# Transposed probabilities of the neighbourhood attention, copied by the scalar and the vector engine in halves

## What is computed

```python
def neighborhood_attention(q, k, v, rpb):
    ...
    qb = q.reshape(B, H, rows, n_cb, Q_BLOCK_W, dh)
    kg = k[:, :, tok]
    vg = v[:, :, tok]
    s = jnp.einsum('bhrnqd,bhrnkd->bhrnqk', qb, kg).astype(jnp.float32) * (dh ** -0.5)
    bias = rpb.astype(jnp.float32)[:, ri, ci]
    s = jnp.where(mask[None, None, None], s + bias[None], NEG)
    p = jax.nn.softmax(s, axis=-1)
    o = jnp.einsum('bhrnqk,bhrnkd->bhrnqd', p.astype(v.dtype), vg)
    return o.reshape(B, H, T, dh)
```

## Time and profile before

| | us |
|---|---|
| median of 3 runs | 1976.39 |
| lowest, highest | 1972.84, 1978.12 |
| profiled execution | 1976.45 |
| its span, first to last instruction | 1974.7 |
| neighbourhood attention, layer 0 | 313.0 to 353.1 |
| neighbourhood attention, layer 1 | 1276.8 to 1317.6 |

### The profile page before, as it was taken

One profiled execution on the slowest core, in us unless ns is written; L12 is line 12 of the kernel. 1 busy time (PEld: TensorE's weight loads), 2 busy tenths in 40 slices (PEclk: granted clock), 3 DMA queues, 4 the chain that ended last, 5 costly groups with the idle time before them and its releaser, 6 DMA issues.

```text
span 1974.7 us, 29955 instructions
## 1 busy us (share of the span) xinstructions
PE 1617.4 (82%) x9962; PEld 972.8 (49%) x9962; DVE 935.2 (47%) x1825; ACT 324.1 (16%) x690; POOL 291.9 (15%) x402
## 2 busy tenths in 40 slices
PE   3998897955997878997849988978399789998874
PEld 1474445853554445554426634467355455554441
DVE  3866757144443333443367476643533344343334
ACT  1242236020000000000032323341000000000000
POOL 0003221001211111121100141300101111111110
PEclk9999998977999999999979999989599999999997
DMA  8951252642999999899488214424369999999995
GB/s 258 312 162 44 85 150 86 256 171 96 381 396 412 405 409 406 358 407 408 191 276 273 75 42 146 154 118 185 131 267 408 408 407 391 412 402 408 410 398 205
DMA packets 150930, 538.59 MB, mean 273 GB/s; under 512 B 16942, under 2 KB 109342, under 8 KB 117566
## 3 DMA queue, kind: packets, MB, share of 16 engines
q1 hardware_dynamic: 135440, 514.17, 67.8%
q0 software_dynamic: 11520, 16.82, 2.6%
q10 hardware_dynamic: 3888, 6.61, 1.0%
HBM read 533.34 MB, written 25.20 MB: 283 GB/s over the span
## 4 chain that ended last, share of the span: by engine, by line
PE 47%; DMA 31%; DVE 8%; issue 6%; SPq 5%; ACT 2%; DVEq 0%; POOL 0%; POOLq 0%; ACTq 0%
PE bank L564 43%; DMA ring<-w 17%; DMA pool_b<-w 7%; DMA pool_a<-xn_rows,tok_now 2%; DMA y_rows<-pool_a,row_now 2%; PE bank L856 2%; DMA pool_b<-b_ada 2%; SPq L430 1%; DVE low L1254 1%; PE bank L878 1%; DVE ring L1433 1%; SPq L415 1%; ACT pool_a L1136 1%; DMA pool_a<-y_rows 1%; SPq L414 1%
## 5 line engine op out<-in xcount | busy, mean ns | idle before, releaser
L564 PE MATMUL bank<-ring,pool_a 128*64 128x256 f32 (+2 forms) x3968 | 557.7, 445 | 112.2 <-DMA ring<-w 67.4
L564 PEld LDWEIGHTS bank<-ring,pool_a 128*64 128x64 f32 (+1 forms) x3968 | 294.7, 143 | 353.3 <-issue 193.8
L564 PE MATMUL bank<-hT,ring 128*128 128x512 f32 (+1 forms) x672 | 304.3, 609 | 32.9 <-DVE pool_b L1418 29.3
L1693 DVE TENSOR_SCALAR pool_a<-pool_a 128x256 f32<-128x256 f32 x72 | 21.4, 297 | 590.2 <-ACT pool_a L1165 590.2
L564 PEld LDWEIGHTS bank<-hT,ring 128*128 128x128 f32 (+1 forms) x672 | 126.9, 192 | 194.2 <-issue 158.2
L1165 ACT ACTIVATE pool_a<-bank 128x256 f32<-128x256 f32 x72 | 27.6, 383 | 1041.5 <-PE bank L564 1041.5
L564 PE MATMUL bank<-ring,hT 128*128 128x256 f32 x768 | 168.6, 380 | 1.9 <-ACT hT L1150 1.9
L564 PEld LDWEIGHTS bank<-ring,hT 128*128 128x128 f32 x768 | 144.9, 190 | 25.7 <-issue 6.4
L1694 DVE RECIPROCAL pool_a<-pool_a 128x256 f32<-128x256 f32 x72 | 126.2, 1753 | 2.5
L1706 DVE TENSOR_TENSOR pool_a<-bank,g_bc 64x512 f32<-64x512 f32 x144 | 99.2, 689 | 40.6 <-PE bank L564 36.4
L564 PE MATMUL bank<-hT,pool_a 128*64 128x256 f32 x768 | 92.8, 396 | 22.0 <-DMA hT<-w 22.0
(11 more groups left out here) (272 smaller groups left out, 1564.1 us busy)
## 6 DMA issues: line engine op xcount, KB each, us to landing
ring<-w SPq DMA_DIRECT2D x129, 2048.0 KB, 26.1
pool_b<-w SPq DMA_DIRECT2D x22, 2048.0 KB, 25.6
hT<-w SPq DMA_DIRECT2D x22, 2048.0 KB, 21.1
low<-w SPq DMA_DIRECT2D x22, 2048.0 KB, 23.0
ring<-w_ada SPq DMA_DIRECT2D x40, 1024.0 KB, 12.1
ring<-w_in SPq DMA_DIRECT2D x24, 1024.0 KB, 5.8
pool_b<-w_ada SPq DMA_DIRECT2D x16, 1024.0 KB
ring<-w_out SPq DMA_DIRECT2D x8, 1024.0 KB, 10.5
```

The lines of the kernel that those rows point to most:

```text
L564: return nc.tensor.matmul(out, lhsT, rhs, start=start, stop=stop, skip_group_check=True)
L1693: own(V.tensor_scalar(e1, e1, 1.0, None, ALU.add), t, 2)
```

## The change

Of the two PSUM tiles of transposed probabilities of each head, the scalar engine goes on copying i = 0, and the vector engine copies i = 1, in its loop two heads after the scores, behind the scaling of the head before. The vector loop gets a tenth turn for the last head. Both engines wait explicitly, from head 2 on, for the product that last read the half of `PT_sb` that they overwrite, and the matrix engine waits for the last copy of each engine before a product. The count order of emptied tiles is adapted.

```diff
         if d >= 1:
-            t += [(("PT", 2 * d - 2 + r, i), "a") for r in range(2) for i in range(2)]
+            t += [(("PT", 2 * d - 2 + r, i), "ad"[i]) for r in range(2) for i in range(2)]
...
             return index[("S", key[1] - 1, 1)] + 0.5
+        if key[0] == "PT" and key[2] == 1 and key[1] < 6:
+            return index[("S", key[1] + 2, 1)] + 0.3
         return index[key]
...
                         d = n - 2
-                        pe.wait_ge(act_took.s, act_took.at(l, taken[("PT", 2 * d + 1, 1)][1]))
+                        pe.wait_ge(act_took.s, act_took.at(l, taken[("PT", 2 * d + 1, 0)][1]))
+                        pe.wait_ge(dve_took.s, dve_took.at(l, taken[("PT", 2 * d + 1, 1)][1]))
...
                     if 2 <= h < 10:
                         g = h - 2
-                        for i in range(2):
-                            b = tile(("PT", g, i))
-                            F(PT_sb[:, g % 2, 2 * i:2 * i + 2, :].rearrange("p c n -> p (c n)"), b[:, :], ACT.Copy
-                              ).then_inc(act_took.s, 1)
+                        b = tile(("PT", g, 0))
+                        if g >= 2:
+                            act.wait_ge(on_done.s, on_done.at(l, g // 2))
+                        F(PT_sb[:, g % 2, 0:2, :].rearrange("p c n -> p (c n)"), b[:, :], ACT.Copy
+                          ).then_inc(act_took.s, 1)
...
-                for h in range(9):
+                for h in range(10):
...
-                    if h >= 1:
+                    if 1 <= h < 9:
                         g = h - 1
...
                         last.then_inc(prob_done.s, 1)
+                    if h >= 2:
+                        g = h - 2
+                        b = tile(("PT", g, 1))
+                        if g >= 2:
+                            dve.wait_ge(on_done.s, on_done.at(l, g // 2))
+                        V.tensor_copy(PT_sb[:, g % 2, 2:4, :].rearrange("p c n -> p (c n)"), b[:, :]
+                                      ).then_inc(dve_took.s, 1)
```

## The result

Over twelve runs each, the changed kernel took 1983.37 us in the median (1976.18 to 1987.99) and the kernel before 1976.71 (1972.00 to 1981.39). The ratio is 1.003 with a 95% interval of 1.0019 to 1.0042, that is +5.9 us, at least 3.8 and at most 8.3 (the two medians lie 6.7 us apart). Measured a second time (first experiment) it was 1.0031. The forecast was +1.8 us, 1978.2 us, with a range up to 1983.0 us. The ratio put on the forecast's starting point of 1976.39 us gives 1982.3 us, near the upper end of that range, and the median of 1983.37 us lies just above it. The sign and the place of the loss were right, the size was too small by a factor of about three.

What follows compares the result with a forecast made beforehand. Bound by one attention stage per layer, scalar engine alternating with matrix engine, vector engine nearly as full. Copy delays less scalar relief gave +0.9 us per layer, +1.8 in all: 1978.2 us, range 1972.0 to 1983.0.

Steps and rivals of the forecast that it cites:

- The stage: Neighbourhood attention, first scores to last output copy, once per layer; its gain or loss is passed on nearly one to one.
- Vector copy 0.65 us: Time charged per moved copy of transposed probabilities on the vector engine; bounds 0.42 and 1.17 us.
- Stand of 0.6 us at head 2, 1.0 us at head 4: Vector engine waits this long for transposes before copying these heads, delaying the scores of heads 5 and 7.
- Head 7's exponentials +1.8: On the scalar engine in layer 0, head 7's exponentials start at 343.8 us against 342.03: 1.8 us later.
- third product +1.3: On the matrix engine in layer 0, the third attention product starts at 346.5 us against 345.20: 1.3 us later.
- fourth +0.9 us: The last attention product, waiting for head 7's vector copy, starts at 351.35 us against 350.48 in layer 0: 0.9 us later.
- rival B: Matrix engine clock low for one more pair's scores, product and transposes: +3.3 us per layer besides 0.9, 1984.8 us; chance 0.11.
- sum of +0.9 us per layer: Net delay of the attention stage in each layer, +1.8 us in all; the forecast's sum, chance 0.60.
- sign named for B: In the new profile, clock at 0.5 in stretches between 334 and 350 us in layer 0.
- Rival A: In the attention stage the vector engine always finds its tile ready: -2.7 us per layer, 1971.0 us; chance 0.13.

Runs made afterwards that it cites:

- first experiment: The changed kernel timed and traced again without any edit, against the kernel before: ratio 1.0031 (1.0019 to 1.0043).
- delayed stage: The kernel before with one idle scalar copy of 2048 columns ahead of the fourth output copy in each layer: ratio 1.0017 (1.0005 to 1.0030).
- even heads: Changed kernel with only the second halves of heads 0, 2, 4 and 6 on the vector engine: ratio 1.0033 over the kernel before.
- filled gap: Changed kernel plus 22 idle transposes on the matrix engine in front of the third product: ratio 1.0009 (0.9997 to 1.0020) over the kernel before.
- odd heads: Changed kernel with only the second halves of heads 1, 3, 5 and 7 on the vector engine: ratio 0.9997 over the kernel before.
- tail heads: Changed kernel with only the second halves of heads 5, 6 and 7 on the vector engine: ratio 0.9996 over the kernel before.
- none moved: Changed kernel with its new waits and loops, but all 32 copies on the scalar engine: ratio 0.9997 (0.9988 to 1.0005) over the kernel before.
- nine fillers: Changed kernel plus nine idle transposes on the matrix engine in front of the third product: ratio 1.0021 (1.0007 to 1.0036) over the kernel before.
- heads 1, 3, 5, 6, 7: Changed kernel with only these heads' second halves on the vector engine, no gap filled: ratio 0.9992 (0.9980 to 1.0005) over the kernel before.

## Why the forecast was right or wrong

- *The stage carries the change; what it loses is passed on.* Right for losses, within the intervals: delayed stage +2.8 us and +3.4 us in time, even heads +6.2 and +6.5 us. For gains see below.
- *Vector copy 0.65 us.* Nearly right: a row takes 688 ns, and the scores start 0.60 us behind its start.
- *Stand of 0.6 us at head 2, 1.0 us at head 4, in front of the scores of heads 5 and 7.* Right: 0.54 and 1.06 us. The matrix engine's own new wait of 1.03 us, twice per layer, was overlooked; the sum came out right without it.
- *Head 7's exponentials +1.8, third product +1.3, fourth +0.9 us.* Right at nearly equal clock: +1.7 and +1.3 us in the repeated trace (layer 0), and +0.9 us for the fourth product as added up under the filled gap. The odd and the even heads show that the place does it.
- *Clock: rival B, 0.11.* Here the forecast failed: the sum of +0.9 us per layer put the clock at nothing. It kept it as a rival, sized by one more pair at the low clock (3.3 us per layer), and called it unlikely, since the kernel before had kept the full level behind a gap as long. The sign named for B, a clock of 0.5 between 334 and 350 us in layer 0, came true (0.50 from 347 to 348 us). In the traces the third product was at the low clock in all four layers of the changed kernel. The term is 1.7 us per layer. That is the forecast's own price for product and transposes (0.5 + 1.1 us, measured 1.6); its third part, 1.7 us for scores, did not come. The kernel before pays for the clock too: its tail was low in layer 1 in two traces of two, at 1.3 us (6.62 instead of 5.28 us from the third to the fourth product). So the clock adds 2 x 1.7 - 1.3 = 2.1 us and the place 2 x 0.9 = 1.8 us, where the stages of the changed kernel are longer by 85.35 - 81.55 = 3.8 us on the mean of two traces each.
- *Rival A, 1971.0 us.* Out, and for the reason given. With A's own idea confined to the odd or the tail heads, the stage does get some 2 us shorter, but each ratio below 1 has an interval that takes in 1.

What stays open is the rest, 5.9 - 3.8 = 2.1 us. The lower end of each of the two intervals, 3.8 us, just reaches the stage's part; as both measurements gave the same ratio, noise alone is not a likely explanation. Part of the rest may be the clock once more: the two other kernels that leave every copy in its place (none moved, stage delayed) had the full clock in both tails, so with the copies left in place the tail was low in two layers of eight and not in every second one, and the mean clock term of the kernel before would be 0.7 us per execution instead of 1.3. Each kernel has one trace, and outside the stage the eleven us between the traces (1888.9 to 1899.7 us of span less stages, in no order that follows the change) hide anything of this size.

The odd and the tail heads are open in the same way: they gained 4.1 and 3.6 us in the traced stages and 0.6 and 0.8 us in time, and their intervals end at 3.0 and 3.4 us. One number on record points at the clock. Over all executions, its granted level averaged 0.933 for the kernel before and 0.932 with none moved, but 0.927 and 0.929 for the changed kernel (measured twice), 0.929 for the odd heads and 0.931 for the tail heads. In the trace of the odd heads the whole span has 0.929 although both tails are full, against 0.934 for before, so the lower level lies outside the tails. What it costs there no run measured, and the even heads (0.931, ratio 1.0033) show that the time does not follow it alone. That a gain in the stage is partly lost behind it is possible and not shown.

## What to carry to other kernels

When work is moved to a second engine, ask what stands behind it there: a copy that waits for its input also holds up everything queued after it, so hand over the pieces whose input is ready when their turn comes, and leave those that would wait. Here that avoided the loss (0.9997 against 1.0033 for the other eight) and made the stage 2.0 us shorter, but no gain in time was clear of its interval: two engines at 6.4 and 6.3 of 7.1 us have little to give each other. And where the matrix engine works in short bursts with gaps of some 3 us, give a clock fall a term in the sum, not only a place among the rivals. That the kernel before stayed at the full level behind one such gap was one layer of one trace; its layer 1 had already fallen.

## What was not expected of the hardware

The granted clock did not follow the length of the last gap. The third product ran at 1.2 GHz behind 2.01 us of idleness (nine fillers) and behind 2.95 us (heads 1, 3, 5, 6, 7), and at 2.4 GHz behind 2.95 us (tail heads) and 3.34 us (kernel before, layer 0). Of the kernels with all 16 vector copies, only the one with the nearly closed gap (0.59 us) was full in both layers. With a gap 25 us earlier filled with 3.06 us of transposes, the third product of the kernel before took 3.30 us in layer 0, where two traces without the filling have 1.97. So the length of the gap alone does not foretell the level; what else decides it was not settled.
